# One call moved in the third mixer's TensorE order: the last state outputs behind the second half of gate block 3

## The reference, cut to what matters

```python
h = rms_norm(x, mix_norm[l])
q_a, k_a, v_a, q_i, k_i, w_i, u_s, q_m, gates = jnp.split(h @ w_in[l], offsets, axis=-1)
...
o_a = indexed_sparse_attention(q_a, k_a, v_a, q_i, k_i, w_i, rel_bias) @ w_o_a[l]
y_s = jax.nn.gelu(s5_layer(u_s, ssm_lambda_re[l], ssm_lambda_im[l], ...))
glu_a, glu_b = jnp.split(y_s @ w_glu[l], 2, axis=-1)
o_b = glu_a * jax.nn.sigmoid(glu_b)
...
o_m = memory_attention(q_m, m_k, m_v) @ w_o_m[l]
g = jax.nn.sigmoid(gates.reshape(b_, s_, N_BRANCHES, D_MODEL))
merged = g[:, :, 0] * o_a + g[:, :, 1] * o_b + g[:, :, 2] * o_m
x = x + merged @ w_out[l]
```

```python
_, _, xr, xi = lax.associative_scan(_complex_affine_combine, elems, axis=1)
y = (jnp.einsum('bsgp,gcp->bsgc', xr, c_re.astype(f32))
     - jnp.einsum('bsgp,gcp->bsgc', xi, c_im.astype(f32))
     + d.astype(f32).reshape(SSM_GROUPS, SSM_GROUP_CH) * uf)
```

## Time and profile before

| | |
|---|---|
| median of 3 runs | 1296.25 us |
| lowest and highest of them | 1294.75 and 1300.05 us |
| the profiled execution's own time | 1297.23 us |
| its span | 1295.4 us |
| PE busy | 1269.0 us, 98% |
| DVE, ACT, POOL busy | 808.7, 639.5 and 278.8 us |
| granted TensorE clock, mean | 0.996 |

### The profile page before, as it was taken

How to read it: one execution, slowest core, us unless ns; L and a number is a source line. 1 busy time by engine, 2 the same in 40 slices (tenths; PEclk the granted TensorE clock), 3 DMA queues, 4 the chain that set the end, 5 groups by cost and what they waited for, 6 DMA issues and landing times.

```text
span 1295.4 us, 19586 instructions
## 1 busy us (share of the span) xinstructions
PE 1269.0 (98%) x7427; PEld 1061.3 (82%) x7427; DVE 808.7 (62%) x1186; ACT 639.5 (49%) x932; POOL 278.8 (22%) x370
## 2 busy tenths in 40 slices
PE   9999999999999999999999999999999999999997
PEld 7996788888799988888888788888887778888886
DVE  4558675555564476654656755556789876755554
ACT  4438654434453365543445654445544683534442
POOL 6520210000000042103000589602276210200000
PEclk9999999999999999999999999999999999999999
DMA  9960555555455655567655655654535336555651
GB/s 302 268 132 19 168 173 191 181 182 192 162 188 172 188 122 163 164 195 183 209 188 162 189 184 182 223 194 136 191 129 163 131 130 195 192 184 193 194 187 41
DMA packets 155997, 224.79 MB, mean 174 GB/s; under 512 B 13508, under 2 KB 108092, under 8 KB 155933
## 3 DMA queue, kind: packets, MB, share of 16 engines
q1 hardware_dynamic: 145248, 212.55, 51.8%
q0 software_dynamic: 10064, 10.54, 4.3%
q10 hardware_dynamic: 620, 0.83, 0.2%
HBM read 222.56 MB, written 1.25 MB: 173 GB/s over the span
## 4 chain that ended last, share of the span: by engine, by line
PE 83%; DVE 7%; ACT 3%; POOL 2%; DMA 2%; issue 2%; DVEq 0%; SPq 0%; POOLq 0%; ACTq 0%
PE bank L223 24%; PE bank L225 24%; PE bank L224 24%; PE bank L244 4%; DVE units_lo L178 2%; PE bank L232 2%; PE bank L747 1%; DMA raw_units<-in_ffn_w_up 1%; ACT arena L1584 1%; PE bank L1000 1%; DVE arena L3099 1%; PE bank L239 1%; POOL rows L1261 1%; DVE arena L3090 1%; DVE arena L2552 1%
## 5 line engine op out<-in xcount | busy, mean ns | idle before, releaser
L666 DVE TENSOR_TENSOR units_lo<-raw_units,units_hi 128x2048 fp32r<-128x2048 f32 x96 | 222.1, 2313 | 154.9 <-ACT units_hi L620 154.9
L223 PE MATMUL bank<-units_hi,turned_hi 128*128 128x512 f32 (+1 forms) x792 | 307.4, 388 | 3.1 <-DVE units_lo L178 1.3
L225 PE MATMUL bank<-units_hi,turned_lo 128*128 128x512 f32 (+1 forms) x792 | 302.3, 382 | 0.0
L224 PE MATMUL bank<-units_lo,turned_hi 128*128 128x512 f32 (+1 forms) x792 | 302.0, 381 | 0.0
L178 DVE TENSOR_TENSOR units_lo<-raw_units,units_hi 128x2048 fp32r<-128x2048 f32 (+2 forms) x101 | 228.4, 2269 | 96.4 <-ACT units_hi L170 96.2
L170 ACT ACTIVATE units_hi<-raw_units 128x2048 fp32r<-128x2048 f32 (+2 forms) x101 | 189.5, 1885 | 100.2 <-PE bank L225 73.2
L620 ACT ACTIVATE units_hi<-raw_units 128x2048 fp32r<-128x2048 f32 x96 | 183.5, 1912 | 104.0 <-PE bank L225 95.6
L223 PE MATMUL bank<-units_hi,second_hi 128*128 128x512 f32 (+1 forms) x560 | 219.2, 391 | 0.0
L225 PE MATMUL bank<-units_hi,second_lo 128*128 128x512 f32 (+1 forms) x560 | 216.8, 387 | 0.0
L224 PE MATMUL bank<-units_lo,second_hi 128*128 128x512 f32 (+1 forms) x560 | 216.6, 387 | 0.0
L223 PEld LDWEIGHTS bank<-units_hi,turned_hi 128*128 128x128 f32 x792 | 149.3, 188 | 32.8 <-DVE units_lo L178 3.0
(11 more groups left out here) (373 smaller groups left out, 1781.2 us busy)
## 6 DMA issues: line engine op xcount, KB each, us to landing
raw_units<-in_ffn_w_up SPq DMA_DIRECT2D x88, 512.0 KB, 4.7
raw_units<-in_ffn_w_in SPq DMA_DIRECT2D x88, 512.0 KB, 4.6
raw_units<-in_ffn_w_down SPq DMA_DIRECT2D x22, 1024.0 KB, 5.0
raw_units<-in_ffn_w_out SPq DMA_DIRECT2D x22, 1024.0 KB, 4.9
raw_units<-in_w_in SPq DMA_DIRECT2D x18, 1024.0 KB, 5.1
raw_units<-in_b_w_q SPq DMA_DIRECT2D x12, 1024.0 KB, 5.2
raw_units<-in_a_w_in SPq DMA_DIRECT2D x9, 1024.0 KB, 11.8
raw_units<-in_kv_w SPq DMA_DIRECT2D x6, 1024.0 KB, 5.3
```

What stands on the lines that cost most here:

```text
L223: pe.matmul(out, lh, rh, start=start, stop=False, skip_group_check=True)
L224: pe.matmul(out, lh, rl, start=False, stop=False, skip_group_check=True)
L225: return pe.matmul(out, ll, rh, start=False, stop=True, skip_group_check=True)
L666: dve.tensor_tensor(m.WL[:, slot(n0 + j), :], m.RAW[:, slot(n0 + j), :], m.WH[:, slot(n0 + j), :].bitcast(F32), ALU.subtract).then_inc(m.l ...
```

## The change

In `mix_c_tensor` two calls change places: the second half of gate block 3 is now issued ahead of the last state outputs. Nothing is added, removed or changed otherwise, and no wait is altered; the streams of DVE, ACT, POOL and SP are the same row for row.

```diff
@@ -2666,8 +2666,8 @@
 def mix_c_tensor(pe, m):
 
     score_pair_c_tensor(pe, m, 0)
+    gate_half_tensor(pe, m, 3, 1)
     state_outputs_tensor(pe, m, 3)
-    gate_half_tensor(pe, m, 3, 1)
     gate_half_tensor(pe, m, 4, 0)
     turn_pair_c_tensor(pe, m, 0)
     score_pair_c_tensor(pe, m, 1)
```

## The result

The change makes the kernel slower by a little: 1299.88 us in the median of 20 runs against 1295.91 us of 20 runs before, a ratio of 1.0028 with a 95% interval from 1.0022 to 1.0034, so 2.9 to 4.4 us. One of the 20 executions of the change was a slow one, 1799.57 us at a mean granted clock of 0.653, and is left out of the ratio. The profiled execution has a span of 1299.6 us, 4.2 more than the 1295.4 of before.

A forecast was written before the change was run, and what follows sets the result against it. PE, 98% busy, was taken to bound the kernel. Transposes 1.55 us later plus 1.7 of low clock made 3.25 us, about 3.2 at the end: 1299.5 us against a median of 1296.25, range 1296.5 to 1302.5 for 8 in 10.

The forecast's parts named there:

- What bounds the kernel, and what the change takes away: PE, 98% busy, bounds; its 2.21 us wait at the state outputs goes, and it reaches pair 0's transposes 3.6 us earlier.
- DVE late by 1.85 us, bounds 1.7 to 1.95: At DVE's state rows (L3107): DVE waits for PE's later state outputs and starts at 1007.26, 1.85 us late.
- Everything up to ACT's scaling follows, with no slack: DVE's and ACT's steps from the state rows to ACT's scaling of pair 0 all move by 1.85 us.
- New wait of 5.2 us, transposes 1.55 us later: At pair 0's transposes: PE arrives at 1012.6, waits for ACT's scaling until 1017.8, 1.55 us later than before.
- The clock behind it, 1.7 us between 0 and 3.4: Behind PE's new wait: half clock costs pair 0's transposes and pair 1's scores 0.85 us each, 1.7 in all.
- another length than 3.4 us: Sign of error: the size is wrong if the clock is at 0.50 for a length other than 3.4 us.
- The rest keeps it: Behind pair 1's scores nothing absorbs the shift, PE's longest later wait being 0.81 us; the end moves by 3.2 us.
- The old gap usually keeps its clock: Rival at the old gap: no 1.5 us credit, sum 4.7 us, 1301.0; 20% together with a longer new low stretch.
- credit: The 1.5 us counted for the change because half clock had followed the old 2.21 us gap.
- the second way of adding up: Check of the sum: -2.21 - 1.5 (old gap and its clock) + 5.2 + 1.7 = 3.2 us.
- the rule of the Trainium skill's page: Activity window free-running, transition varying between runs; the old gap's low stretch, 1.5 us of credit, would be missing in some executions.
- The second gap at pair 1: Rival at pair 1's transposes: PE stops again and pays a wait and low stretch, 6.9 us, 1303.2; 5%.

The follow-up runs named there:

- the run with DVE alone late: PE's order of before, with one DVE index round moved from behind the bias of pair 0 to ahead of the state rows; ratio 1.0013 against before.
- the filled run: The changed order plus 20 matmuls whose result nobody reads in PE's new wait ahead of the transposes of pair 0; ratio 1.0016 against before.
- The filled gap of before: The order of before plus 8 matmuls whose result nobody reads in the old gap ahead of the last state outputs; ratio 0.9999 against before.
- the split order: Against before: state outputs placed between the two row tiles of the gate half, ratio 1.0008; with 13 unread matmuls filling PE's wait at the transposes, 1.0009.
- the cover back: The changed order plus 24 more gate matmuls ahead of the transposes of pair 0, with DVE and ACT steps reordered; ratio 1.0017 against before.
- the scores first: Split gate half, scores of pair 1 ahead of pair 0's transposes, 6 unread matmuls; 1.0000 against before, 0.9990 with ACT's block 4 tanh ahead of unit g0+11.
- the cover back with the tanh early: The restored-cover kernel, with ACT's tanh of block 5 and upper part of the first sums ahead of pair 2's scaling and unit g0+13; 0.9993 against before.

## Why the prediction was right, point by point

*What bounds the kernel, and what the change takes away.* Right. PE's wait of 2.21 us went, the outputs started 6.73 us behind the scores (forecast 6.7), and the gate half had no wait for its unit.

*DVE late by 1.85 us, bounds 1.7 to 1.95.* L3107 moved from 1005.41 to 1007.34, 1.93, less the 0.18 inherited, 1.75. Inside the bounds. I had PE ready for the release at 1007.06 and took 0.2 for the hop; measured from PE's outputs, 1006.21 + 1.06 = 1007.27 to 1007.34, it was 0.07.

*Everything up to ACT's scaling follows, with no slack.* Right, and the run with DVE alone late shows it by itself: 1.32 us there gave 1.29.

*New wait of 5.2 us, transposes 1.55 us later.* 5.02 and 1.53.

*The clock behind it, 1.7 us between 0 and 3.4.* Here the size was off, and by the prediction's own sign ("another length than 3.4 us") it was wrong in this term. The stretch at half clock lasted 6.8 us in all, 5.6 of them after PE took up work, where the one of the earlier trace rows had lasted 3.4, so that it ran on into the gate matmuls. That is the doubling that the upper bound had allowed for. At the first of them I was still right, 1021.83 - 999.48 = 22.35 against 19.08, 3.27 for the forecast 3.25; another 0.76 came in the next two microseconds. From transposes to transposes the loss is 2.5 us in place of 1.7; by the filled run 2.3 of it are the clock, and the other 0.2 are there at full clock too, since the second head waits for the fourth scaling step.

*The rest keeps it.* Right: +4.03 at the transposes of pair 1 and +4.00 at the wait of the earlier trace rows, and 4.2 at the end of the span with the 0.18. In the medians it is 3.97, by the ratio 3.6; I forecast 3.2, 1299.5, and it was 1299.88. That the two times lie within 0.4 us is part luck: I had started from a median of three runs, 1296.25, and that of 20 is 1295.91. The profiled execution of the change, 1301.41, also lies 1.5 above its median, so its low stretch need not be the usual one. And 20 runs of each could tell 0.28% from nothing, where I had put the limit at 0.5%.

*The rivals.* None of them decided, and one was priced wrongly, as the runs show. "The old gap usually keeps its clock" I put at 1.5 us more: I had subtracted the old low stretch as a credit. The filled gap of before shows that this stretch was worth nothing (0.02 us in the distance), because the same chain set the start of the transposes with it or without it. My own sum did not need the credit (1.55 + 1.7 counts from the transposes); the second way of adding up, with the old gap's 2.21 and 1.5, came out alike because the new wait is counted from an arrival that is earlier by just these. And the rule of the Trainium skill's page "TensorE: Matmul & The Clock Gate", section "What's actually happening", that I had set against the credit, therefore could not have changed the result: the profile of the kernel with the state rows late shows the low stretch behind the same gap once more, but its absence would have been free. "The second gap at pair 1" did not come: the copies of the turned pair ended at 1021.36, and the exp of pair 1 waited for DVE's bias, not for them.

## What to carry to other kernels

A wait on the busiest engine is not its cost: follow what the engine waits for next, and take the difference at that release. Here 3.6 us of gap and low clock were free, since PE next met a chain on DVE and ACT that was ready at most 0.2 us before it came, and the call that was moved to close the gap was the head of that chain. When calls are reordered, count for each release how much work stands between it and its use, on both sides, and give back the cover that was taken; then read the other engines' orders at the next places that are reached early, because there the gain is lost again.

## What the runs showed of the hardware

How long the clock stays low behind a wait varied: 3.4 us after PE's restart in the kernel before (a gap of 2.21), 5.6 in the changed one (a gap of 5.02). In the latter it had fallen 1.2 us before PE took up work, so it was low for 6.8 us in all. In the split order, with a wait of 3.29, the clock fell only after PE had taken up work again, at about 1015.6, for 3.4 us. In this part of the mixer it did not fall behind waits of 0.90, 1.05, 1.17, 1.56 and 1.86 us. Yet near 355 us, where PE waits 1.24 and then 0.82 us in every one of the fourteen profiles, three of them have a low stretch of 3.4 us right behind and the others none. So the lengths of the waits alone do not tell the cases apart here.

More surprising is a low stretch in code that no version touches. Near 81 us, with PE busy, the profiles of the change and of before and five others have it for about 3.4 us, five have none (the split order without and with filling, the change and before with filling, the cover back), and two have 6.8: the scores first and the cover back, both with the tanh early. The rows of the latter by stretch:

```profile
80.00:81.00 1.00, 1.00 (x11) 0.96 0.05 1
81.00:82.00 1.00, 1.00 (x6) 0.50 0.30 52
...
87.00:88.00 1.00, 1.00 (x8) 0.63 0.92 254
```

The scores of pair 0, some 900 us later, start at 997.39 to 998.26 in the five profiles without it, at 998.55 to 999.92 with 3.4 us of it, and at 1001.22 and 1002.00 in the two with 6.8, which also have the one near 355. That is why spans of single profiles (1293.5 for the filled gap of before, 1297.2 for the cover back with the tanh early) say nothing here, and why I compared distances inside the mixer. The Trainium skill, in the page "TensorE: Matmul & The Clock Gate", section "What's actually happening", has the window as free-running and the transition as varying between runs. These rows agree on the variation, from 0 to 6.8 us at half clock for the same instructions; what it comes from they do not show.
